# A mixture-of-experts step: the rows of experts 0 to 7 through a slot-ordered buffer in DRAM and an indirect gather

## The reference, cut to what matters

```
pg = softmax(t @ wg + bg); g = argmax(pg)              # 4 groups, top 1
le_g = (t @ we + be) of group g                        # 4 experts in it
v, idx = top_k(softmax(le_g), 2); v = v / sum(v)       # top 2
comb = one_hot(4 g + idx, 16) * p_top * v              # weight of each expert
hid = silu(t @ w_gate[e]) * (t @ w_up[e]) * comb       # width 512
out = sum over e of hid @ w_down[e]                    # width 1024
x = layer_norm(ALPHA * x + g2 * out)
```

## Time and profile before

| | us |
|---|---|
| median of 3 runs | 486.19 (484.97 to 486.24) |
| profiled execution | 485.3 |
| its span | 483.2 |

### The profile page before, as it was taken

One profiled execution on the slowest core, in us unless ns is written; L12 is line 12 of the kernel. 1 busy time (PEld: TensorE's weight loads), 2 busy tenths in 40 slices (PEclk: granted clock), 3 DMA queues, 4 the chain that ended last, 5 costly groups with the idle time before them and its releaser, 6 DMA issues.

```text
span 483.2 us, 6512 instructions
## 1 busy us (share of the span) xinstructions
PE 446.0 (92%) x2394; PEld 239.7 (50%) x2394; DVE 238.6 (49%) x448; ACT 121.5 (25%) x242; POOL 63.0 (13%) x61
## 2 busy tenths in 40 slices
PE   2678999999999999799999999999999999998882
PEld 1244555556654456595554454455554444553420
DVE  3552713848743347951124153454445545536767
ACT  2400168682230225352111110111111111121200
POOL 2000024356550421021000000000000000000300
PEclk9989999999999999999999999999999999998988
DMA  8999996855999026801999899999999999997003
GB/s 231 383 387 387 288 387 236 305 217 187 323 378 366 15 84 265 320 30 33 363 387 420 366 340 393 390 431 427 425 419 420 425 429 423 416 429 301 1 2 130
DMA packets 32611, 146.90 MB, mean 304 GB/s; under 512 B 3688, under 2 KB 4520, under 8 KB 24376
## 3 DMA queue, kind: packets, MB, share of 16 engines
q1 hardware_dynamic: 31376, 143.40, 76.3%
q10 hardware_dynamic: 1032, 2.81, 1.5%
q0 software_dynamic: 160, 0.10, 0.3%
HBM read 144.72 MB, written 1.58 MB: 303 GB/s over the span
## 4 chain that ended last, share of the span: by engine, by line
PE 75%; SPq 11%; DVE 6%; issue 3%; ACT 2%; DMA 1%; POOLq 1%; POOL 0%; DVEq 0%; ACTq 0%
PE PS L1805 19%; PE PS L1845 11%; PE PS L1671 9%; PE PS L1569 8%; PE PS L1812 6%; SPq L420 5%; PE PS L1875 5%; PE PS L1746 4%; SPq L425 3%; PE PS L1497 2%; PE PS L1546 2%; PE PS L1852 1%; PE PS L1603 1%; PE PS L1882 1%; PE PS L1827 1%
## 5 line engine op out<-in xcount | busy, mean ns | idle before, releaser
L1805 PE MATMUL PS<-ring,xs 128*64 128x256 f32 x896 | 102.9, 382 | 0.0
L1805 PEld LDWEIGHTS PS<-ring,xs 128*64 128x64 f32 x896 | 61.8, 137 | 36.8 <-issue 8.3
L1569 PE MATMUL PS<-hT,ring 128*128 128x388 f32 x192 | 67.5, 502 | 2.6 <-DVE hT L902 2.6
L1227 DVE SCALAR_TENSOR_TENSOR y<-PS,comb,y 128x1024 f32<-128x1024 f32 x42 | 53.5, 1277 | 0.3 <-PE PS L1882 0.3
L1845 PE MATMUL PS<-ring,hTs 128*64 128x512 f32 x224 | 52.9, 616 | 0.0
L1569 PEld LDWEIGHTS PS<-hT,ring 128*128 128x128 f32 x192 | 36.7, 194 | 31.6 <-issue 8.3
L1176 DVE SCALAR_TENSOR_TENSOR hid<-sg,PS 128x256 f32<-128x256 f32 x18 | 10.7, 612 | 46.8 <-PE PS L1805 36.0
L1458 POOL TENSOR_TENSOR y<-y,g2r 128x1024 f32<-128x1024 f32 x1 | 2.4, 2373 | 234.4 <-DVE y L1227 234.4
L1845 PEld LDWEIGHTS PS<-ring,hTs 128*64 128x64 f32 x224 | 15.3, 141 | 31.3 <-issue 31.2
L738 ACT CAST yh<-PS 128x512 fp32r<-128x512 f32 x13 | 7.6, 585 | 89.0 <-PE PS L1845 55.1
L1214 DVE TENSOR_TENSOR yl<-PS,yh 128x512 fp32r<-128x512 f32 x13 | 9.0, 692 | 41.9 <-ACT yh L738 41.9
(11 more groups left out here) (272 smaller groups left out, 601.6 us busy)
## 6 DMA issues: line engine op xcount, KB each, us to landing
ring<-in_ex_w_gate SPq DMA_DIRECT2D x16, 2048.0 KB, 12.0
ring<-in_ex_w_up SPq DMA_DIRECT2D x16, 2048.0 KB, 14.0
ring<-in_ex_w_down SPq DMA_DIRECT2D x16, 2048.0 KB, 12.7
ring<-in_w_ada SPq DMA_DIRECT2D x11, 2048.0 KB, 11.9
ring<-in_w_in SPq DMA_DIRECT2D x2, 2048.0 KB, 23.2
ring<-in_w_out SPq DMA_DIRECT2D x2, 2048.0 KB, 10.3
ring<-in_w_ada SPq DMA_DIRECT2D x2, 1024.0 KB, 14.9
ring<-in_w_in SPq DMA_DIRECT2D x2, 1024.0 KB, 14.7
```

What stands on the lines that cost most here:

```text
L1227: dve.scalar_tensor_tensor(out=y, in0=src, scalar=comb[:, i, e:e + 1], in1=y, op0=ALU.mult, op1=ALU.add).then_inc(s["acc_done"], 1)
L1569: mm = pe.matmul(PS[:, w % 4, 0:W], wt[:, k, (w % 4) * P:(w % 4 + 1) * P], hT[:, k, :], start=(k == 0), stop=(k == KD - 1))
L1805: mm = pe.matmul(PS[HALF * h:HALF * (h + 1), bank, 0:FE // 2], x(k, HALF), w[:, k, h * (FE // 2):(h + 1) * (FE // 2)], start=(k == 0), sto ...
```

## The change

Experts 8 to 15 stay as they were. For experts 0 to 7 (`BY_ROWS = 8`) nothing is combined on TensorE. ScalarE's `rows_out` copies an expert's output out of PSUM and writes its rows into a DRAM buffer `slot_rows`, at the expert's first slot. Writes of 64 or 128 rows run over into the next expert's slots and are overwritten by it, so each waits for the one before. When all eight are out, POOL gathers for every token tile the row of each token's first and of its second expert, six indirect DMAs of 128 rows of 4 KB, by `rowid`. VectorE's `row_sum` adds the two, each times its weight, into `y12`; on it experts 8 to 14 add as before. A token whose expert is 8 or above (or whose row is past an expert's first 128) gets row 896, which holds zeros: SP fills the whole buffer (912 rows) with zeros ahead of time. `project_out(e)` then waits for `row_sb2` (the copy of the expert before) up to e = 8, and `y_out(8)`, which overwrites the buffers of the gather, for `sum_done`.

Routing: `first_max` runs once over all five blocks (group logits and four groups of expert logits); the products with the group mark are put off; `rowid` is made ahead of `gap_done`. On TensorE the 12 matmuls on `pw` stand ahead of the first dispatch.

The diff, cut (waits that only count from expert 8 on, renamed scratch and renumbered semaphores are left out):

```
+BY_ROWS = 8
+EMPTY = NSLOT + CAP
+        part = [at("part0", A0, [P, D]), at("part1", A0 + 4096, [P, D])]
+        slot_rows = nc.dram_tensor("slot_rows", (EMPTY + 16, D), F32).ap()
@@ SP, expert loads
+                if v == 1:
+                    sp.dma_start(slot_rows[:, :], t["empty"].partition_broadcast(EMPTY + 16)).then_inc(s["empty_in"], 16)
@@ ACT
+            def rows_out(e):
+                used(act, unit(e, 2))
+                need(act, "row_out", 32 * e)
+                if e == 0:
+                    act.wait_ge(s["disp_sb"], 2 * KD)
+                    act.wait_ge(s["empty_in"], 16)
+                off = offs[e]
+                def few():
+                    act.copy(part[0][:, 0:512], PS[:, 3, :]).then_inc(s["row_sb2"], 1)
+                    act.wait_ge(s["row_sb2"], e + 1)
+                    for h in range(2):
+                        act.dma_start(slot_rows[bass.ds(off, HALF), 512 * h:512 * (h + 1)],
+                                      part[0][HALF * h:HALF * (h + 1), 0:512]).then_inc(s["row_out"], 16)
+                def many():
+                    act.copy(part[0][:, :], PS[:, 3:5, :].rearrange("p a n -> p (a n)")).then_inc(s["row_sb2"], 1)
+                    act.wait_ge(s["row_sb2"], e + 1)
+                    for h in range(2):
+                        act.dma_start(slot_rows[bass.ds(off, CAP), 512 * h:512 * (h + 1)],
+                                      part[0][:, 512 * h:512 * (h + 1)]).then_inc(s["row_out"], 16)
+                fork(act, counts[e], few, many)
@@ y_out
+                if e == BY_ROWS:
+                    act.wait_ge(s["sum_done"], NT)
@@ ACT, expert loop
-                y_out(e)
+                (rows_out if e < BY_ROWS else y_out)(e)
@@ DVE, routing
-            first_max(gl, C_COD4, og, rs[:, 0, :], rt[:, 5, :, 0:NG], rs[:, 11, :])
-            first_max(by_group(el), C_COD4, oh14, mx1, tmp4, top)
+            first_max(by_group(lg[:, :, :]), C_COD4, by_group(oh5[:, :, :]), mx5, by_group(mark5[:, :, :]), top5[:, 1])
...
-            step(dve.tensor_tensor(oh14, oh14, og4, ALU.mult))
-            link(dve.tensor_tensor(oh24, oh24, og4, ALU.mult))
-            dve.tensor_tensor(asg, oh1, oh2, ALU.add).then_inc(s["assign_done"], 1)
-            link(dve.tensor_tensor(rt[:, 4], oh1, oh2, ALU.add))
+            link(dve.tensor_tensor(pair, first, oh2, ALU.add))
+            dve.tensor_tensor(by_group(asg), by_group(pair), og4, ALU.mult).then_inc(s["assign_done"], 1)
+            link(dve.tensor_tensor(by_group(pair), by_group(pair), og4, ALU.mult))
...
+            step(dve.tensor_tensor(by_group(oh1), by_group(first), og4, ALU.mult))
+            step(dve.tensor_tensor(by_group(oh2), by_group(oh2), og4, ALU.mult))
             low_part(1)
@@ DVE, ahead of gap_done
+            far, inv = rs[:, 4:6, :], rs[:, 6:8, :]
+            for j, oh in enumerate((oh1, oh2)):
+                link(dve.tensor_tensor(rt[:, 6], oh, off.unsqueeze(1).broadcast_to([P, NT, NE]), ALU.mult))
+                link(dve.tensor_reduce(far[:, j, :], rt[:, 6], AX.X, ALU.add))
+            link(dve.tensor_tensor(far, pw[:, :, :], far, ALU.subtract))
+            link(dve.tensor_scalar(far, far, float(CAP), None, ALU.is_ge))
+            link(dve.tensor_scalar(inv, pw[:, :, :], totoff[:, 1, BY_ROWS:BY_ROWS + 1], None, ALU.is_ge))
+            link(dve.tensor_tensor(inv, inv, far, ALU.max))
+            link(dve.tensor_scalar(far, pw[:, :, :], -1.0, float(EMPTY), ALU.mult, ALU.add))
+            link(dve.tensor_tensor(inv, inv, far, ALU.mult))
+            dve.tensor_tensor(rowid[:, :, :], pw[:, :, :], inv, ALU.add).then_inc(s["rowid_done"], 1)
@@ DVE, experts
+            def row_sum(i):
+                dve.wait_ge(got_in[i], 32)
+                y = y12[:, i, :]
+                dve.tensor_scalar(y, y, wk[:, 0, i:i + 1], None, ALU.mult).then_inc(s["got_done"], 1)
+                dve.wait_ge(s["got_done"], i + 1)
+                dve.scalar_tensor_tensor(out=y, in0=part[i % 2][:, :], scalar=wk[:, 1, i:i + 1], in1=y,
+                                         op0=ALU.mult, op1=ALU.add).then_inc(s["sum_done"], 1)
@@ DVE, expert loop
-                if e:
+                if e > BY_ROWS:
                     gather(e - 1, 0)
                 hidden(e + 1)
-                choose(e)
-                if e:
+                if e >= BY_ROWS:
+                    choose(e)
+                if e == BY_ROWS:
+                    for i in range(NT):
+                        row_sum(i)
+                if e > BY_ROWS:
                     gather(e - 1, 1)
-                y_low(e)
-                if e:
+                if e >= BY_ROWS:
+                    y_low(e)
+                if e > BY_ROWS:
                     gather(e - 1, 2)
@@ POOL, after the state output
+            pool.wait_ge(s["rowid_done"], 1)
+            pool.wait_ge(s["row_out"], 32 * BY_ROWS)
+            for i in range(NT):
+                for j, dst in enumerate((y12[:, i, :], part[i % 2][:, :])):
+                    if i == 2 and j == 1:
+                        pool.wait_ge(s["sum_done"], 1)
+                    pool.indirect_dma_start(dst, None, slot_rows, bass.IndirectOffsetOnAxis(ap=rowid[:, j, i:i + 1], axis=0))\
+                        .then_inc(got_in[i], 16)
@@ project_out
-                need(pe, "yh_done", e)
-                need(pe, "yl_done", e)
+                if e <= BY_ROWS:
+                    need(pe, "row_sb2", e)
+                else:
+                    pe.wait_ge(s["yh_done"], e - BY_ROWS)
+                    pe.wait_ge(s["yl_done"], e - BY_ROWS)
```

More of the change, by code:

```diff
@@ L163, in build @@
         cnt = keep("cnt", [P, 1 + NE + PASSES * NE], I32)
+        rowid = keep("rowid", [P, 2, NT], I32)
         wr = keep("wr", [P, KD, 32])
@@ L169, in build @@
         rt = keep("rt", [P, 8, NT, NE])
+        oh5 = at("oh5", router0, [P, NT, NG + NE])
+        mark5 = at("mark5", router0 + 256, [P, NT, NG + NE])
+        top5 = at("top5", router0 + 512, [P, 2, NT, 5])
         stq = at("stq", place[0], [P, 24])
@@ L276, in p1_loaded @@
             eng.wait_ge(ring_in[slot], 16 * ((u + 1) // RING + (slot > 0)))
+        slot_rows = nc.dram_tensor("slot_rows", (EMPTY + 16, D), F32).ap()
+        got_in = [sem(f"got_in{i}") for i in range(NT)]
         block = ctx.enter_context(nc.Block())
@@ L1075, in _ @@
-            link(dve.scalar_tensor_tensor(out=rt[:, 7], in0=oh1, scalar=-2e30, in1=el, op0=ALU.mult, op1=ALU.add))
-            first_max(x4, C_COD4, oh24, mx2, tmp4, top)
+            mx5 = top5[:, 0]
+            first_max(by_group(lg[:, :, :]), C_COD4, by_group(oh5[:, :, :]), mx5, by_group(mark5[:, :, :]), top5[:, 1])
+            mx0, mx1 = mx5[:, :, 0], mx5[:, :, 1:]
+            og, first = oh5[:, :, 0:NG], oh5[:, :, NG:]
+            oh1, oh2, pair, asg = rt[:, 4], rt[:, 5], rt[:, 6], marks16[:, :, :]
@@ L1077, in _ @@
+            mx2, top = rs[:, 0:4, :].rearrange("p a i -> p i a"), rs[:, 4:8, :].rearrange("p a i -> p i a")
+            link(dve.scalar_tensor_tensor(out=rt[:, 7], in0=first, scalar=-2e30, in1=el, op0=ALU.mult, op1=ALU.add))
+            first_max(by_group(rt[:, 7]), C_COD4, by_group(oh2), mx2, by_group(rt[:, 4]), top)
             og4 = og.unsqueeze(3).broadcast_to([P, NT, NG, EPG])
-            step(dve.tensor_tensor(oh14, oh14, og4, ALU.mult))
-            link(dve.tensor_tensor(oh24, oh24, og4, ALU.mult))
@@ L1140, in _ @@
                 dve.tensor_scalar(io[:, q, :], io[:, q, :], -1.0, None, ALU.add).then_inc(s["io_done"], 1)
-            step(dve.tensor_tensor(rt[:, 5, :, 0:NG], gl, wide(rs[:, 0, :], NG), ALU.subtract))
-            link(dve.tensor_tensor(rt[:, 4, :, 0:NG], mx2, mx1, ALU.subtract))
-            link(dve.tensor_tensor(rt[:, 4, :, 0:NG], rt[:, 4, :, 0:NG], og, ALU.mult))
-            link(dve.tensor_reduce(rs[:, 4, :], rt[:, 4, :, 0:NG], AX.X, ALU.add))
+            far, inv = rs[:, 4:6, :], rs[:, 6:8, :]
[9 more added lines that the diff above has]
+            dve.tensor_tensor(rowid[:, :, :], pw[:, :, :], inv, ALU.add).then_inc(s["rowid_done"], 1)
+            gaps, over, gap = mark5[:, :, 0:NG], mark5[:, :, NG:2 * NG], rs[:, 8, :]
+            step(dve.tensor_tensor(over, gl, wide(mx0, NG), ALU.subtract))
+            link(dve.tensor_tensor(gaps, mx2, mx1, ALU.subtract))
+            link(dve.tensor_tensor(gaps, gaps, og, ALU.mult))
+            link(dve.tensor_reduce(gap, gaps, AX.X, ALU.add))
             dve.nop().then_inc(s["gap_done"], 1)
@@ L1196, in choose @@
                     dve.wait_ge(s["disp_sb"], 2 * KD)
-                need(dve, "selT_done", e)
-                need(dve, "c_ps", NT * (e - 1))
+                n = e - BY_ROWS
+                need(dve, "selT_done", n)
+                need(dve, "c_ps", NT * (n - 1))
                 def rows_of(q):
@@ L1750, in dispatch @@
                     mm.then_inc(s["disp_ps"], 1)
-            pe.wait_ge(s["h2lo"], 2)
-            pe.wait_ge(s["x1_done"], NT)
-            for i in range(NT):
```

(7 more changed lines are left out.)

95 lines of the change are left out of this document (47 added, 48 removed).

## The result

The changed kernel takes 508.14 us (median of 4, 507.69 to 512.74) against 485.58 before: 1.049 times as long, interval 1.045 to 1.054. Its profiled execution has a span of 505.9 us against 483.2.

What follows compares the result with a forecast made beforehand. TensorE bound the kernel, with DMA full too and only 4.9 us of load lead left. Span 483.2 + 11.4 (later combine(8, 0)) + 1.7 (clock) = 496.3, as a median of runs 499 us; own range 492 to 506, 8 in 10 482 to 514.

Steps and rivals of the forecast that it cites:

- rival (b): Gathers before combine(8, 0) slower still: 44 us of movement gives 510 us, rows cut in 2 KB packets 530; chance 0.14.
- Routing, 1.5 us: Ahead of the experts: one first_max instead of two gains 0.8 us, the moved pw matmuls 0.7; bounds 0 and 2.2.
- Expert 7's projection over at 335.0: End of expert 7's output projection on TensorE: from 353.2 to 336.5 by saved combines, to 335.0 with routing.
- Combines off TensorE, bounded by the loads: Experts 0 to 7: 18.7 us of TensorE saved, but expert 14's load leaves only 4.9 us to gain.
- rival (a): Quick gathers: 7.4 to 15 us of movement, end 483.3, or 479 with free row writes; chance 0.28.
- Zero fill hidden, 8.8 us or 17.6: SP queue before the experts' waiting loads: 3.7 MB take 8.8 us, hidden; at half rate 17.6, nearly all hidden.
- Rows landed at 343.3: Expert 7's row writes, before the gathers: from 335.0, copy 0.6, issues 0.7, packets 5, landing 2.0 us.
- T: Start of combine(8, 0), the first combine left on TensorE: forecast 382.0, 11.4 us later than before.
- rival (c): Rows held up at ScalarE: its tanh 1 to 3 us late in experts 4 and 5; 487 to 490; chance 0.08.
- Gather packets 33.3 us: Six gathers beside weights: 48 packets per engine, each waiting for one weight packet, 33.3 us; bounds 7.4 and 44.
- Clock 1.7 us: TensorE right behind its 28 us gap: clock granted at 0.57 for the next 4 us, costing 1.7 us.
- T + 112.6 us, loads not late: From combine(8, 0) to the end: same work as before; expert 14's gate load lands at 416.7, wanted only at 432.7.

Runs made afterwards that it cites:

- e1: Changed kernel with BY_ROWS = 0: only the new routing and moved pw matmuls kept, all experts combined on TensorE; 482.13 us against 484.96 for the kernel before.
- e3: Changed kernel without the DMAs of the row writes, copies kept, so gathers read zeros and start behind expert 7's copy; 493.48 us, 1.019 times the kernel before.
- e2: Changed kernel without the six gathers and row_sum, row writes and fill kept, POOL clears y12; 477.79 us, 0.986 times the kernel before.
- e5: Changed kernel with a 128-row region for each expert and two copy buffers, so a write waits only for that two experts back; 502.82 us.
- e4: Changed kernel with weight loads 22 to 36 each issued as four DMAs of 4 KB runs; 489.27 us, 1.011 times the kernel before.
- e10: Changed kernel with 38 extra matmuls, result unused, filling TensorE's gap before combine(8, 0); 503.91 us, 1.041 times the kernel before.
- e7: Changed kernel with both own row regions per expert and loads 22 to 36 in 4 KB pieces; 488.71 us, 1.009 times the kernel before.
- e6: Changed kernel with SP holding back load 30 and all behind it until all six gathers have landed; 492.83 us, 1.015 times the kernel before.

## Why the prediction was right

The direction and the mechanism held: a way of dependent transfers, slow by packet counts, longer than its cover. The number fits less well than the wide range of 482 to 514 makes it look. 508.14 lies outside the forecast's own 492 to 506, the gap was 35.8 us where 25 to 32 were to show it, and 508 lies nearest to the 510 of rival (b), whose mechanism didn't come. The sum was 9 us short, and the steps before the gathers are where.

- **Routing, 1.5 us.** The first load that waits for TensorE left 2.4 us earlier in the changed kernel, just past the bound of 2.2, and 1.6 in e1; with the same routing it left up to 2.5 us later in other runs. e1's medians give 2.8 us, of which part may be the tail. The sign is right, the size is not settled.
- **Expert 7's projection over at 335.0.** It was, but by two slips that cancel: the start brought 2.4 us and not 1.5, and from there the saved combines brought 15.8 and not 16.7. The waits for hTs, 1.3 us, were put at nothing, and combine(6, 2), 0.66 us, was counted though it stands behind that projection. Not counted was that projections with no combine behind them often took some 0.15 us less (3.45 instead of 3.60); in e3, where nothing waits, it is 17.5.
- **Combines off TensorE, bounded by the loads.** Right: in e2 they bring 4.2 to 4.4 us, where I had read 4.9 from the load of expert 14. The 479 of rival (a) with free writes stands against 477.8 measured, but its own terms (2.9 + 6.2 = 9.1 us earlier) give 477, and e2 has the writes and not the gathers.
- **Zero fill hidden, 8.8 us or 17.6.** It took 26.1 us to land. The window 210 to 212 us has q1 at 0.41 MB in 2 us with the engines over full: 205 GB/s, half of a weight load's. That was the case of half the rate, some 18 us, and it moved behind the load of up ahead of it, which landed only at 207.0. It ended at 224.2, just before load 7 was issued at 224.5: hidden, with 0.3 us left.

```profile
q1 hardware_dynamic: 100, 0.41, 114.7%
```

- **Rows landed at 343.3.** This is the step that failed: the rows landed at 350.97, so it is 7.7 of the 9.75 us that T is over its 382.0. I had expert 7's copy start at the end of its projection. It started 4.6 us later, behind the writes of expert 6. I knew the wait (rival (c)) but priced it as a delay of ScalarE's tanh in experts 4 and 5, 1 to 3 us, and not as a queue: an expert up to 64 rows takes 11.2 us of TensorE, while the copies, each behind the landing of the one before, followed each other after 11.7, 10.7 and 11.5 us. So the 5.0 us by which expert 3's 512 KB made expert 4's copy late (projection over at 300.7, copy at 305.67) were never worked off. The rest, 3.1 us, is mostly the landing itself: 9.96 us from issue, where I had 5 for packets and 2 for landing, as the first packet moved only some 4 us after the issue. e5 shows the first part: without the order the copies follow their projections at once. There the weights took part of it back, so its price on T is between 2.6 and 4.6 us. e3 shows the two together with the rest of the way.
- **Gather packets 33.3 us.** From 356 to 387, 31: right, by the right rule (equal packet counts; e4 changes the weight packet and the time follows). The ring holds seven loads and not the eight I counted; they sufficed. The first of them came later than forecast, near 356 for an issue at 351.8, so that the last landed 36.6 us after the rows instead of 35.3.
- **Row sum, copy, low part 3.4 us.** 4.2 from the last landing to combine(8, 0).
- **Clock 1.7 us.** 1.7 by e10, with a gap of 35.8 instead of 28 us. The level is right; that the size fits to a tenth is luck, as e3, e4, e5 and e7 paid 2.1 to 3.2 us at the same place.
- **T + 112.6 us, loads not late.** 114.2, which is the 1.7 of the clock, with a tail as slow as before; behind the gap TensorE waits for no load. Right here, but only as the gap fills the ring: in e6, with T at 371.5, loads decide.
- **Rivals.** (a) Quick gathers would have decided the sign. Its point, 20.2 us of movement, stood on rows landed at 343.3; in e4 they landed at 346.0, with 21.7 us from the first gather's issue to the last landing, and T = 372.9 is 2.3 us too late, 1% slower. In e6 the gathers are quicker still, and T is 0.9 us too late; from there the loads held back decide. (b) 44 us didn't come. (c) was no rival but a term of the sum. Its effect on TensorE is there too, 0.7 and 0.6 us of wait for hTs in experts 5 and 6.

The Trainium skill (DMA: Bandwidth & Descriptors, Anatomy of one DMA) fits a GpSimd DMA at 2.0 us plus bytes over 436 GB/s. My estimate from it, about 9 us, takes the six gathers as one transfer. Measured: 14.3 with the engines to themselves (e6), 35.7 beside full queues.

## What to carry to other kernels

Beside a full queue price a transfer by its packets times the neighbour's packet, not by its bytes, and add the wait for its first packet; and where a result goes out to DRAM and comes back, add up the whole way from the last producer to the first user and hold it against the work that covers it, here some 57 us of way (335.0 to 391.75) against 21 us of cover. If such a way has to be, short packets for the bulk loads around it gave back 19 of 23 us here, at nearly the same rate; the kernel was still 1% slower than before. A buffer whose writes each wait for the one before is a queue: compare its period with the producer's, and ask where a single long one is ever made up for.

## What was not expected of the hardware

- The fill, one 4 KB row in DRAM written to 912 rows in DRAM, moved 205 GB/s at full engines, half the 420 to 430 GB/s of weight loads. Whether that is the target or the one source row no run here tells.
- The first packet of a newly issued DMA came some 4 us after the issue beside full queues (ScalarE's at 340.34, POOL's at 351.82), and 1.6 to 1.8 us after it in e6 with empty ones.
- 2 MiB loads in 4 KB packets moved 408 to 414 GB/s by themselves (332 to 338 us in e4) and 415 together with the gathers, little below the 420 to 430 of longer ones. But SP was held 4 to 9 us at each load of four DMAs but the first and last, against 0.33 us for one DMA:

```profile
333.99 5.96 SPq L460 DMA_DIRECT2D ring<-in_ex_w_gate  x4
```
